# A two-block transformer kernel in one launch: residual turns, norm chunks and two-head attention batches re-ordered

## The reference, cut to what matters

```python
def layer_norm(x, g, b):
    mu = mean(x); var = mean((x - mu)**2)
    return (x - mu) * rsqrt(var + LN_EPS) * g + b
# first network, layer i (0 and 1), its last lines:
h = layer_norm(DN_ALPHA * h + 0.5 * swiglu(h, ...), ...)
h = h + (p[i] @ ple_w_proj[i]) * sigmoid(h @ ple_w_gate[i])
# second network
h = rms_norm(x, norm_mix_g)
# 8 heads of 64 in 2 groups, three branches each: 31 compressed keys, selected blocks
# (all keys up to the query, since the top 8 of 8 blocks are taken), a window of 256 keys
o_a = g0 * compressed + g1 * selected + g2 * window
# 8 more heads of 64: a window of 128 keys, with sinks
mix = (gate_a * (o_a @ w_a) + gate_b * (o_b @ w_b)) @ w_o
x = x + mix
x = x + hier_moe(rms_norm(x, norm_ffn_g), ...)   # 32 experts, 2 of them for each token
return rms_norm(x, norm_final_g)
```

## Time and profile before

| | us |
|---|---|
| median of three runs | 3364.46 |
| the profiled execution, its own time | 3364.31 |
| its span in the trace | 3362.5 |
| network 1, up to the end of norm ple1 (about) | 2443 |
| second network up to its attention | 2443 to 2586 |
| attention of the second network, wide heads and sliding heads | 2586 to 2779 |
| merge and output | 2779 to 3001 |
| last norm and ranking | 3001 to 3052 |
| experts and final norm | 3052 to 3362 |

### The profile page before, as it was taken

One profiled execution on the slowest core, in us unless ns is written; L12 is line 12 of the kernel. 1 busy time (PEld: TensorE's weight loads), 2 busy tenths in 40 slices (PEclk: granted clock), 3 DMA queues, 4 the chain that ended last, 5 costly groups with the idle time before them and its releaser, 6 DMA issues.

```text
span 3362.5 us, 31721 instructions
## 1 busy us (share of the span) xinstructions
PE 3136.2 (93%) x12846; PEld 2170.7 (65%) x12846; DVE 1392.2 (41%) x3041; ACT 471.0 (14%) x1020; POOL 316.2 (9%) x304
## 2 busy tenths in 40 slices
PE   9999999889999999999997999999899989997774
PEld 7886446738888858888643478888365654453221
DVE  6563212426553426553558365543321780121112
ACT  1101010011000110010122210000211550011001
POOL 0000100110000100001012300001001550011010
PEclk9999998799999999999998999999999999988998
DMA  5222212012222212222121122222122001226997
GB/s 196 87 76 81 94 75 75 13 63 82 88 88 88 88 63 101 88 87 89 54 75 38 38 94 88 86 90 88 63 100 113 1 1 63 75 88 251 373 396 299
DMA packets 54200, 344.34 MB, mean 102 GB/s; under 512 B 7968, under 2 KB 8096, under 8 KB 15520
## 3 DMA queue, kind: packets, MB, share of 16 engines
q1 hardware_dynamic: 44352, 318.79, 25.4%
q10 hardware_dynamic: 5088, 15.05, 1.2%
q0 software_dynamic: 4608, 8.40, 0.7%
HBM read 335.92 MB, written 14.68 MB: 104 GB/s over the span
## 4 chain that ended last, share of the span: by engine, by line
PE 84%; DVE 7%; DMA 6%; POOL 1%; issue 1%; ACT 1%; SPq 1%; ACTq 0%; DVEq 0%; POOLq 0%
PE bank L777 44%; PE bank L469 24%; DMA ring<-in_weights 6%; PE bank L478 4%; PE bank L2427 2%; PE bank L1412 2%; PE bank L499 1%; PE bank L505 1%; POOL area L1752 1%; PE bank L1634 1%; PE bank L1656 1%; PE bank L1439 1%; DVE stat L1701 1%; DVE area L1946 1%; PE bank L585 1%
## 5 line engine op out<-in xcount | busy, mean ns | idle before, releaser
L469 PE MATMUL bank<-area,ring 128*128 128x512 f32 (+1 forms) x1220 | 452.4, 532 | 33.4 <-DVE area L1542 15.6
L469 PEld LDWEIGHTS bank<-area,ring 128*128 128x128 f32 x1220 | 213.8, 193 | 267.5 <-issue 231.1
L777 PE MATMUL bank<-buf_a,mixed 128*128 128x256 f32 x1408 | 320.2, 380 | 0.0
L777 PE MATMUL bank<-buf_b,mixed 128*128 128x256 f32 x1408 | 319.2, 379 | 0.0
L777 PEld LDWEIGHTS bank<-buf_a,mixed 128*128 128x128 f32 x1408 | 268.0, 190 | 36.7 <-DVE mixed L807 0.4
L777 PEld LDWEIGHTS bank<-buf_b,mixed 128*128 128x128 f32 x1408 | 267.6, 190 | 36.3
L469 PE MATMUL bank<-buf_b,ring 128*128 128x512 f32 x656 | 285.1, 593 | 0.7 <-ACT area L2115 0.7
L799 DVE TENSOR_TENSOR mixed<-ring 128x512 f32<-128x512 f32 (+1 forms) x124 | 84.1, 678 | 466.5 <-PE bank L777 460.0
L777 PE MATMUL bank<-buf_a,ring 128*128 128x256 f32 x1056 | 246.3, 383 | 9.1 <-DMA buf_a<-in_x 7.3
L777 PE MATMUL bank<-buf_b,ring 128*128 128x256 f32 x1056 | 245.3, 382 | 1.8 <-ACT buf_b L668 1.8
L777 PE MATMUL bank<-area,mixed 128*128 128x256 f32 x1056 | 233.8, 379 | 0.0
(11 more groups left out here) (351 smaller groups left out, 3275.2 us busy)
## 6 DMA issues: line engine op xcount, KB each, us to landing
ring<-in_weights SPq DMA_DIRECT2D x300, 1024.0 KB, 4.8
area<-chosen SPq DMA_DIRECT2D x8, 512.0 KB, 6.9
buf_a<-in_x ACTq DMA_DIRECT2D x4, 512.0 KB, 7.7
turn_tables<-area ACTq DMA_DIRECT2D x4, 512.0 KB, 2.6
area<-turn_tables ACTq DMA_DIRECT2D x4, 512.0 KB, 4.7
tokens<-area ACTq DMA_DIRECT2D x4, 512.0 KB, 3.5
out<-area ACTq DMA_DIRECT2D x4, 512.0 KB, 2.6
const<-in_const ACTq DMA_DIRECT2D x1, 1498.0 KB, 13.4
```

Source lines behind the costliest of these rows:

```text
L469: mm = pe.e.matmul(bank[0:w.shape[1], 0:n], w, x[k], start=k == 0, stop=k == len(pieces) - 1)
L777: mm = pe.e.matmul(b, w[:, k * P:(k + 1) * P], x(INPUT_OF[p], unit.lo + k), start=(unit.key, BANK_OF[p]) not in begun, stop=unit.last and ...
```

## The change

1. Norms. In the layer norms `ffn0, ab, ffn2, c`, PE issues 6 products of 128 columns that nobody reads (12 passes) after spreading the means and 6 after spreading the scale; in `ple1` 6 and 3.
2. `ffn1` and `ffn3`. The planner keeps the projections off the banks of the means and of the scale, and ACT copies one of the last four projections after every second chunk of L668.
3. Attention, in general. PE's step has the order scores, values, turns instead of scores, turns, values; banks are given from three fixed pools; ACT moves a finished head out before it copies turned groups.
4. Attention of the second network. Steps of two items, the same queries of a head of group 0 and one of group 1. PE alternates between the two in the scores (on row halves) and in the values (on column halves). DVE copies only the first group of the first item, ACT the rest. Both heads of a tile are moved out at once. There are 6+6 slots for weights and 8 for turned ones instead of 4+4 and 5, and one output bank instead of two.
5. Residual turns. Blocks 0 and 1 are turned while the scale of norm `nsa` is made, block 2 after the scale is spread, block 3 before `rank`. ACT: the first half copy of `xt` stands ahead of the square root; the first exponential stands after block 0 of `xr`, the second after block 1.

```diff
     def plan_mean(st, beside=None):
         i = NORMS.index(st)
+        order = [(g.turn + j) % 8 for j in range(8)]
         g.add(("mean", st), (mean_read, i + 1))
         g.add(("squares", st), (square_read, STATS[st] + 1))
+        g.add(("means", st), (means_read, i + 1))
+        if beside is None:
+            plan_scales(st)
+            return
+        others = itertools.cycle(order[4:] + order[:2])
+        for m in range(KD):
+            if m == KD // 2:
+                plan_scales(st, order[3])
+            beside(m, next(others))
+        g.turn = next(others)
...
+    def idle_products(pe, label, read, n):
+        pe.wait_ge(*read)
+        for _ in range(n):
+            pe.e.matmul(bank(label)[:, 0:P], C("ident"), C("mean"), start=True, stop=True)
...
+    def scalar_ln(ac, st, src, dst, at, beside=None):
...
+            if beside and n % 2:
+                beside(ac, n // 2)
...
         def tensor(self, pe):
+            for s in range(-1, len(self.batches) + 3):
...
+                for i, k, br, last in self.score_steps(self.batch(s + 1)):
+                    b = opened(pe, g, (self.name, "s", i, k))
+                    mm = pe.e.matmul(b[:, br["at"]:br["at"] + br["n"]], br["q"], br["k"], start=True, stop=True)
...
+                for j, steps in enumerate(zip(*lists)):
+                    for i, (out, w, p) in zip(self.batch(s - 3), steps):
+                        mm = pe.e.matmul(out, w, p, start=j == 0, stop=j == len(lists[0]) - 1)
...
+                for i in self.batch(s - 2):
...
+                            mm = transpose(pe, b[:, c:c + P], item["slot"][k][:, c:c + P])
...
+                      1, lambda i, n: (n + i) % 2, ((0, 1, 2), (3, 4, 5), (6, 7)))
...
+                      2, lambda i, n: i % 2 == 0 and n == 0, ((0, 1, 2, 3), (4, 5, 6), (7,)))
...
+    XT_ROOT, XT_SCALE, XT_RANK = (0, 1), (2,), (3,)
     def tensor_route(pe, stream, h, ready, r):
         x = cols(h)
+        tensor_turn_residual(pe, r, XT_SCALE)
         tokens_product(pe, stream, g, [("router", b) for b in range(TB)], plan["router"][0], x, NGRP + NEXP, ready)
         for b in range(TB):
             tensor_turn_tokens(pe, g, "xr", h, b)
+        tensor_turn_residual(pe, r, XT_RANK)
...
-        for b in range(TB):
-            tensor_turn_tokens(pe, g, "xt", r, b)
...
     def scalar_route(ac, before):
         ac.e.dma_start(gain, io["gain"]).then_inc(gain_loaded, 16)
+        scalar_turn_half(ac, "xt", xt, xt_done, 0, 0)
+        scalar_rms_sqrt(ac, "nsa")
+        scalar_turn_half(ac, "xt", xt, xt_done, 0, 1)
+        scalar_turn_tokens(ac, "xt", xt, xt_done, (1, 2))
+        rows(0)
         ac.wait_ge(route_diff, 1)
         ac.e.activation(ge, ge, ACT.Exp).then_inc(route_exp, 1)
+        rows(1)
         ac.wait_ge(route_diff, 2)
         ac.e.activation(r_w[:, :, 1:2], r_m, ACT.Exp).then_inc(route_exp, 1)
-        for b in range(TB):
-            scalar_turn_tokens(ac, "xt", xt, xt_done, b)
+        rows(2)
+        rows(3)
+        scalar_turn_tokens(ac, "xt", xt, xt_done, XT_RANK)
```

## The result

The changed kernel takes 3310.51 us in the median of four runs (3301.69 to 3312.27), the kernel before beside it 3365.71: a ratio of 0.9828, 95% interval 0.9805 to 0.9851. That is 55 us less, where 57 had been forecast (3307). The profiled execution took 3312.27 us with a span of 3310.4, against 3362.5 before, so the two traces have to account for 52.1 us.

What follows compares the result with a forecast made beforehand. The chain was 84% PE, with gains only where PE waits or runs at half clock. Terms 18.1 + 7 - 1 + 22 + 10.8 = 56.9 us gave 3307 us; forecast range 3292 to 3318, eight in ten 3286 to 3336.

Steps and rivals of the forecast that it cites:

- Projections: Norms ffn1 and ffn3: with the banks kept apart PE runs on at full clock; gains 8.6 and 9.5, together 18.1 us.
- Idle products: Norms ffn0, ab, ffn2, c, ple1: unread products keep the clock up; 7 us gained, between 14.6 gained and 10 lost.
- I take half: Five norms with idle products: of 14.6 us lost to half clock, about half, 7 us, was forecast as gain.
- First attention: First network's attention: values ahead of turns may wait for ACT's copy; loss 1 us, between gain 3 and loss 4.
- Second attention: Second network's attention: overlapping halves relieve PE, DVE ends last, 25 us a wide pair instead of 31.1; gain 22 us.
- DVE's wait for turns: Second attention, wide heads: DVE waits for PE's values and turns, 0.5 us a step, 2 us a pair.
- The factor of the overlap: Second attention: alternating halves cut PE's time for scores and values to 0.6, giving 9.7 us a head.
- PE is the bound, DVE close behind: Second attention before the change, wide heads: PE needs 14.2 of 15.55 us a head, DVE 12.5.
- The partly fallen clock: Rival, second attention: two of four wide pairs run at half clock, giving 3326 us; chance 0.20.
- The rival without overlap: Second attention: halves don't overlap in short products, PE still bounds wide heads, 8 gained instead of 22, 3321; chance 0.08.
- Last norm and ranking: Norm nsa to the experts' start: later root, faster router, earlier exponential, clock, branch beside gather: -1.7+3+3.7+1+4.8 = 10.8 us.
- Do turns keep the clock up?: Router behind the last norm: turns were taken to keep the clock up; the opposite rule, 3 us less, got 1 in 10.

Runs made afterwards that it cites:

- serial kernel: Changed kernel, but in the second network's attention PE takes scores and values of one kv half, then the other, instead of alternating; 3324.55 us, ratio 0.9876.

## Why the prediction was right, point by point

**Projections: right**, 8.6 and 9.5 us as worked out. PE runs from the means' spread through projections into the gate without a pause (1167.53, 1174.40), at 0.43 us a pass. ACT's mixed order didn't show up in the chain.

**Idle products: the step "I take half" failed.** The five losses added up to 14.6 us; 12.9 came back in the trace, and taking the products away cost 14.1. The clock held in every layer norm of the changed kernel's trace, also in ab and c, where a wait of 1.7 to 1.9 us for the mean has no set in it. The cost that I had set against it, a set at half clock that stands into the wait, needs a clock that has fallen. In that trace it had not; in three of the experiments it had, in just these two norms, and the cost was 0.9 to 1.1 us in each.

**First attention: wrong, -6.6 instead of -1, and outside the bound of -4.** I had seen the wait (values for ACT's copy) and priced it at 0.3 us, 8 times. That was right: a head takes 0.33 us more. Where the clock stayed up, the new order cost 1.4 us in all, close to the forecast. What the sum had at nothing is the clock in the drain at the end. It fell to 0.50 there, which cost 2.5 us in the drain and 2.7 in the products behind it. Undoing the order gave 6.15 us back, and the clock fell only in traces with the new order, though not in all of them (five of seven). Why it fell in those and not in the other two isn't shown.

**Second attention: 19.7 instead of 22, a loss and two surpluses.** By ACT's move-outs the pairs behind the first took 27.87, 30.24 and 22.54 us (the last one runs into the sliding heads), 80.65 together where the same outputs took 92.23 before. That is 11.6 gained, where three times 6.1 had been forecast. The first pair, for which nothing was taken, came 3.7 us sooner, and the sliding heads with the drain gave 4.4 instead of 2. The failed term is DVE's wait for turns. It was put at 0.5 us a step, 2 a pair; it was 4.05. Values and turns ahead of DVE's group were taken as 2.6 to 3.1 us, against 2.0 to 2.7 of DVE's own. Taking the values out of that row removed the wait, and the clock stayed at 1.00 through the wide heads of that run. The factor of the overlap, 0.6 by analogy, was right for both: 0.58 for the values (0.059 against 0.102) and 0.55 for the scores (5.3 against 9.7 us), only that the scores don't need the alternation for it. "PE is the bound, DVE close behind" overrated PE. In the kernel before the chain of one wide head, 15.5 us, left PE for 6.5 us, mostly for DVE and this piece:

```profile
2635.47 2.82 POOL area L1752 x3
```

And with turns first and no alternation a pair takes 24.8 us. POOL doesn't stand in the forecast as a bound at all, and it was the leading one in two of the experiments.

**The partly fallen clock** was a rival with a chance of 0.20. It was 0.94, 0.94 and 0.88 in three stretches of 28 us in the changed kernel's wide heads, 0.82 in those of the experiment with the first attention's order, 1.00 with turns first. So a small part of it happened, inside the forecast. The rival without overlap (3321) comes near the time of the serial kernel, 3324.55, but by luck: it had PE as the bound with 28.4 us a pair, where the pair took 31.1, and 24.8 with turns first.

**Last norm and ranking: 12.2 instead of 10.8.** The root came 1.7 us later, from 2.66 to 4.36, as charged. The router gained 3.3, where 3 were taken. The branch lies beside the gather, as shown by putting the turns back. Between the router and the gather 6.8 us were gained, where 3.7 for DVE's earlier exponential and 1 for the clock had been taken; this is the surplus. The gather itself took 5.23 us instead of 4.30, which is spread: 4.28 to 5.50 in the experiments that have it behind the same code.

**Do turns keep the clock up?** The prediction gave 1 in 10 to the rule that they don't. With 24 turns around the root and the spread the router ran at a mean granted clock of 0.67 and took 10.54 us; without them at 0.50 and 13.89. In all ten traces with the turns in their new places it took 9.23 to 11.23 us. The two windows, changed kernel and turns last:

```profile
2965.43:2975.96 10.53, 10.53 (x65) 10.53 (x66) 5.41 (x14) 0.62 (x2) 0.00 (x0) 0.67 0.01 2
```

```profile
2968.31:2982.20 13.89, 13.89 (x65) 13.89 (x66) 5.50 (x14) 0.00 (x0) 0.00 (x0) 0.50 0.01 1
```

The Trainium skill ("TensorE: Matmul & The Clock Gate", Part 4: PE-mode transpose) states that the full clock doesn't engage for transposes. For these float32 turns this case's runs disagree, by 3.3 us in one router.

**Still open:** why the wide heads of some executions run at 0.82 and of others at 0.94 with the same code, why the drain of the first attention and the norms ab and c keep the clock in some and not in others, and why the products behind the second attention took 166.17 instead of 165.08 us in the changed kernel. None of these was tried by itself.

## What to carry to other kernels

When an engine takes its work in a fixed order, ask of each piece who waits for it, and put the piece with the impatient reader first. The turns had DVE waiting, the values only a move-out that nobody needed; one exchanged order was worth 16 us in the traces, 19 by the ratios, about a third of the whole change. In the first attention the same exchange was worth 1.4 us, and 5.2 more where the clock fell. So look at the drain of a stage too: what a low clock there costs the products behind it can be more than the waits that one priced.

When a faster engine stops being the bound, its remaining gain lies in how soon it answers the engine that is: alternating the halves was worth up to 15 us ahead of the turns and 5 behind them.

## What the runs showed of the hardware

- Products on the two column halves (the values) overlap down to 0.059 us a pass of 128 columns in float32 when they alternate, and take 0.102 when the same passes stand in two blocks. On the two row halves (the scores) both orders overlap: 24 passes of 384 columns took 5.3 us alternating and 5.8 in two blocks, against 9.7 with one half at a time. A wait between the blocks took the overlap away (1.99 us for each six passes, against 2.24 for twelve).
- The router's 64 passes of 36 columns ran at 0.50 from the first to the last, PE busy all the time, where the clock was down when they began: 13.84 and 13.89 us. In the changed kernel it was at 1.00 when they began and fell partway: 10.54 us at 0.67. Over the ten traces like it they took 9.23 to 11.23 us.
- ACT's load of a function table (1.28 us) stands directly ahead of the activation that needs it, but ahead of that one's own wait. With the root in its old place it ran during PE's sums (2.66 us from addition to root). Behind another wait or the issue of a transfer it lay in the chain (3.55), behind a copy more so (4.36).
- Sets of 12 idle passes of 128 columns in the norms' waits held the clock in the norms ab and c in seven of ten traces, and not in three.
- The branch into the experts costs PE 4.5 to 4.8 us of "issue" behind the last copy it waits for. When that copy is done before the gather (4 to 5 us) begins, PE starts 0.14 us behind the gather's landing.
